# Second block: gate products in eight 384-column tiles, latents' products over two pairs of PSUM banks, first products of a turned tile reordered, bias rows turned one tile later

## The reference, cut to what matters

```python
c_act = jax.nn.silu(c)                                  # c: (1, 1024)
ada = c_act @ w_ada[l] + b_ada[l]                       # w_ada[l]: (1024, 6144)
sh1, sc1, gt1, sh2, sc2, gt2 = jnp.split(ada, 6, axis=-1)
```

```python
h = rmsnorm(x, ln_mix_g[l])
proj = h @ w_in[l]                                      # 1024 x 4128
ya = dilated_window_attention(qa, ka, va, bias_a)       # 8 heads of 64
yb = differential_attention(q1, q2, k1, k2, vb, lam, bias_b)   # 4 heads, two softmaxes each
qc = rmsnorm(cq, mla_q_norm_g[l]) @ w_uq[l]             # 768 x 768
kvc = rmsnorm(ckv, mla_kv_norm_g[l]) @ w_ukv[l]         # 256 x 1024
yc = mla_attention(...)                                 # 8 heads
gates = jax.nn.sigmoid(h @ w_gate[l] + b_gate[l])       # 1024 x 3072
merged = gates[0] * (ya @ w_br_a[l]) + gates[1] * (yb @ w_br_b[l]) + gates[2] * (yc @ w_br_c[l])
x = x + merged @ w_o[l]
```

## Time and profile before

| what | value |
|---|---|
| median of 3 runs | 1841.11 us (1839.01 to 1841.4) |
| time of the profiled execution | 1840.13 us |
| its span | 1838.3 us |
| PE / DVE / ACT / POOL busy | 96% / 69% / 48% / 3% |
| HBM read, mean rate | 343.69 MB, 188 GB/s |
| mean granted TensorE clock | 0.998 |

### The profile page before, as it was taken

The page is one execution under the profiler, slowest core; times in us unless marked ns, Lnnn a source line. Parts: engine busy times, 40 slices in busy tenths (PEclk is TensorE's granted clock), DMA queues, the critical chain, the costliest instruction groups (busy, mean ns, idle before and its releaser), DMA issues.

```text
span 1838.3 us, 26917 instructions
## 1 busy us (share of the span) xinstructions
PE 1761.9 (96%) x9090; PEld 1427.5 (78%) x9090; DVE 1272.3 (69%) x1949; ACT 889.8 (48%) x1506; POOL 55.7 (3%) x111
## 2 busy tenths in 40 slices
PE   7999999998999999999999999999999999999998
PEld 3775778986766789988987677788789877778886
DVE  5688897668788875566547887555555578865555
ACT  1456335443465344444655664444455556544443
POOL 0000010000000000002000000000000000000000
PEclk9999999999999999999999999999999999999999
DMA  8866568764765576645664334555556643345553
GB/s 306 260 222 207 178 223 291 257 218 147 236 220 193 182 233 210 209 158 155 190 217 156 119 98 149 187 180 183 179 166 181 219 137 126 112 150 186 183 181 128
DMA packets 212237, 346.12 MB, mean 188 GB/s; under 512 B 19915, under 2 KB 97273, under 8 KB 211881
## 3 DMA queue, kind: packets, MB, share of 16 engines
q1 hardware_dynamic: 208760, 338.89, 57.1%
q0 software_dynamic: 1632, 5.39, 1.0%
q10 hardware_dynamic: 1746, 0.54, 0.1%
HBM read 343.69 MB, written 1.07 MB: 188 GB/s over the span
## 4 chain that ended last, share of the span: by engine, by line
issue 80%; PE 12%; DVE 4%; DVEq 1%; POOLq 1%; POOL 1%; ACT 1%; DMA 0%; SPq 0%; ACTq 0%
PE acc L150 2%; PE acc L148 2%; PE acc L149 2%; PE prod L199 1%; PE prod L200 1%; PE prod L201 1%; DVE w_lo L134 1%; PE prod L148 1%; PE prod L150 1%; PE prod L149 1%; DVEq L908 1%; DVE proj L909 1%; DVE x_res L909 0%; DVE x_res L907 0%; ACT w_hi L128 0%
## 5 line engine op out<-in xcount | busy, mean ns | idle before, releaser
L134 DVE TENSOR_TENSOR w_lo<-w_raw,w_hi 128x1024 fp32r<-128x1024 f32 (+3 forms) x568 | 642.0, 1150 | 337.9 <-ACT w_hi L128 332.9
L128 ACT CAST w_hi<-w_raw 128x1024 fp32r<-128x1024 f32 (+3 forms) x568 | 556.3, 992 | 423.7 <-PE acc L150 171.5
L148 PE MATMUL prod<-w_hi,hT_hi 128*128 128x512 f32 (+1 forms) x880 | 331.1, 376 | 8.6 <-ACT proj_b L1912 2.2
L150 PE MATMUL prod<-w_hi,hT_lo 128*128 128x512 f32 (+1 forms) x880 | 323.1, 367 | 0.0
L149 PE MATMUL prod<-w_lo,hT_hi 128*128 128x512 f32 (+1 forms) x880 | 322.0, 366 | 0.0
L148 PEld LDWEIGHTS prod<-w_hi,hT_hi 128*128 128x128 f32 x880 | 165.7, 188 | 41.2 <-DVE w_lo L134 8.2
L150 PEld LDWEIGHTS prod<-w_hi,hT_lo 128*128 128x128 f32 x880 | 165.8, 188 | 24.0
L149 PEld LDWEIGHTS prod<-w_lo,hT_hi 128*128 128x128 f32 x880 | 166.3, 189 | 21.2
L148 PE MATMUL prod<-w_hi,uT_hi 128*128 128x512 f32 x368 | 152.1, 413 | 10.8 <-DVE w_lo L134 7.7
L150 PE MATMUL prod<-w_hi,uT_lo 128*128 128x512 f32 x368 | 145.8, 396 | 0.0
L149 PE MATMUL prod<-w_lo,uT_hi 128*128 128x512 f32 x368 | 145.7, 396 | 0.0
(11 more groups left out here) (332 smaller groups left out, 2681.5 us busy)
## 6 DMA issues: line engine op xcount, KB each, us to landing
w_raw<-in_w_in_dram SPq DMA_DIRECT2D x72, 512.0 KB, 3.8
ada_raw<-in_w_ada_dram SPq DMA_DIRECT2D x68, 512.0 KB, 7.0
w_raw<-in_w_in_dram SPq DMA_DIRECT2D x192, 172.0 KB, 2.4
w_raw<-in_w_up_dram SPq DMA_DIRECT2D x64, 512.0 KB, 4.3
w_raw<-in_w_down_dram SPq DMA_DIRECT2D x64, 512.0 KB, 4.7
w_raw<-in_w_gate_dram SPq DMA_DIRECT2D x96, 256.0 KB, 3.1
w_raw<-in_w_ffn_gate_dram SPq DMA_DIRECT2D x88, 256.0 KB, 3.5
w_raw<-in_w_ffn_up_dram SPq DMA_DIRECT2D x88, 256.0 KB, 4.3
```

The lines of the kernel that those rows point to most:

```text
L128: act.copy(self.hi[:, s, 0:cols], self.raw[:, s, 0:cols]).then_inc(self.hi_done, 1)
L134: dve.tensor_tensor(self.lo[:, s, 0:cols], self.raw[:, s, 0:cols], self.hi[:, s, 0:cols].bitcast(F32), ALU.subtract).then_inc(self.lo_done, 1)
L148: pe.matmul(out, a_hi, w_hi, start=first and c == 0, stop=False)
L150: mm = pe.matmul(out, a_lo, w_hi, start=False, stop=last and c == chunks - 1)
```

## The change

Six edits, all in the order or the width of work; what is computed is the same.

1. `w_gate` is cut into eight tiles of 384 columns (`GW`), one for each of the eight pairs and heads of A and B. Beside each stand four groups of 12 products. In B the next head's q and k are turned after the second group, and the probabilities after the third. PE's loop over the pairs of A is written out.
2. The tiles of `w_uq` go to `acc[0:2]` and `acc[2:4]`, those of `w_ukv` to `prod` and `acc[2:4]` (`up_banks`). The wait before them and the three identity products are gone. The turn of the first pair's probabilities, which writes to `acc[2:4]`, waits for the second `w_ukv` tile to be taken.
3. Layer 0: the fifth `w_in` tile runs before the eight bias rows are reversed, its weights are loaded before `flip`, the bias rows and the vectors, and the eight identity products are gone. The other four rows are reversed after the sixth tile; ACT's and DVE's copies move along.
4. `part_in_turn`, used at all eight turned tiles: within a group the two high-by-high products come first and wait only for the high parts, then two with the weight's low part, then two with the low part of the turned rows.
5. c is loaded with eight neighbouring values to a partition, and chunk k of `w_ada` is rows 8 p + k: neighbouring partitions read rows that lie eight rows apart. Each descriptor is as long as before.
6. `take_tile` is given its banks.

```diff
+    def part_in_turn(self, pe, pos, lhs, k0, width, tok, out, first, last, hi_taken, lo_taken):
+        if tok == 0:
+            pe.wait_ge(self.hi_done, pos.count(1 + self.groups))
+        if hi_taken:
+            hi_taken()
+        for c in range(KG):
+            pe.matmul(out, a_hi[c], w_hi[c], start=first and c == 0, stop=False)
+        if tok == 0:
+            pe.wait_ge(self.lo_done, pos.count(RING + 1 + self.groups))
+        for c in range(KG):
+            pe.matmul(out, a_hi[c], w_lo[c], start=False, stop=False)
+        if lo_taken:
+            lo_taken()
+        for c in range(KG):
+            mm = pe.matmul(out, a_lo[c], w_hi[c], start=False, stop=last and c == KG - 1)
...
+            def ada_chunks(l, k, chunks, cols):
+                return dr["w_ada"][slice(l, l + 1), :, cols].rearrange("a (p k) n -> p (a k) n", p=P)[:, k:k + chunks, :]
...
-            act.dma_start(c_col[:, :], dr["c"].rearrange("a (k p) -> p (a k)", p=P),
-                          allow_slow_non_contiguous=True).then_inc(first_in, 16)
+            act.dma_start(c_col[:, :], dr["c"].rearrange("a (p k) -> p (a k)", p=P)).then_inc(first_in, 16)
...
+GW, GATES = 3 * D // (PAIRS + BH), PAIRS + BH
+        up_banks = [acc[0:2], acc[2:4], prod, acc[2:4]]
...
                 for t in range(LAT_TILES):
                     in_tile(IN2_T - LAT_TILES + t, layer(l, 4 * t, G2))
+                in_tile(0, layer(l, 4 * LAT_TILES, G2))
                 if l == 0:
                     sp.wait_ge(first_left, 1)
                     sp.dma_start(flip, dr["flip"]).then_inc(consts_in, 16)
...
-                with sp.Fori(0, 6) as t:
+                with sp.Fori(0, GATES) as t:
                     for g in range(4):
-                        rows(Pos(G2_GATE + g, (l, G2), (t, 4)), ws["w_gate"], g * KG * P, bass.ds(t * NT, NT), NT)
+                        rows(Pos(G2_GATE + g, (l, G2), (t, 4)), ws["w_gate"], g * KG * P, bass.ds(t * GW, GW), GW)
...
# vector, branch B
-                    split(nxt + (-1), 2)
+                    split(nxt + (-1), 1, KG * GW)
+                    split(nxt, 2, KG * (GW if b < BH - 1 else NT))
                     if b > 0:
                         branch_b_lo(b - 1)
-                    if b % 2:
-                        add_gate_bias(gate_tile(l, 4 + b // 2), nxt + (-3), slice(2 * D + b // 2 * NT, 2 * D + (b // 2 + 1) * NT))
+                    split(nxt + 2, 1, KG * (GW if b < BH - 1 else NT))
+                    add_gate_bias(gate_tile(l, PAIRS + b), nxt + (-1), slice((PAIRS + b) * GW, (PAIRS + b + 1) * GW))
...
# tensor
-                    reverse_bias(range(4))
-                    T.awake(pe, layer(l, F2_LAT, F2), 8)
...
+                tile(layer(l, 4 * LAT_TILES, G2), layer(l, LAT_TILES, N2), uT, 0, 4, IN2_W)
+                if l == 0:
...
+                    reverse_bias(range(4))
+                tile(layer(l, 4 * LAT_TILES + 4, G2), layer(l, LAT_TILES + 1, N2), uT, 0, 4, IN2_W)
...
-                vacated(layer(l, N2_UQ, N2))(0)
-                for _ in range(3):
-                    pe.matmul(prod[0][:, 0:SEQ], ident, ident.unsqueeze(1).to_broadcast([P, 2, P]), start=True, stop=True)
...
-                with pe.Fori(0, PAIRS) as t:
+                for t in range(PAIRS):
...
-                    W.multiply(pe, this, uT, 4 * e, NT, KG, outs(NT), e == 0, False,
-                               vacant=vacated(gate_tile(l, 4 + b // 2)) if e == 0 else None)
+                    W.multiply(pe, this, uT, 0, GW, KG, outs(GW), True, False, vacant=vacated(gate_tile(l, PAIRS + b)))
+                    W.multiply(pe, this + 1, uT, 2, GW, KG, outs(GW), False, False)
                     if b < BH - 1:
                         qk_turns(n + 1, qk_turn(l, m + 1))
...
+                    W.multiply(pe, this + 2, uT, 4, GW, KG, outs(GW), False, False)
...
-                    W.multiply(pe, this + 1, uT, 4 * e + 2, NT, KG, outs(NT), False, e == 1, between=turn_p)
+                    W.multiply(pe, this + 3, uT, 6, GW, KG, outs(GW), False, True)
```

More of the change, by code:

```diff
@@ L165, in multiply, with turned_tile @@
                 between()
-    def turned_tile(self, pe, pos, lhs, width, outs, turn, taken, vacant, awake, before, after):
+    def turned_tile(self, pe, pos, lhs, width, outs, turn, taken, vacant, awake, before, after, halved):
         awake(0, before)
@@ L248, in awake, with halved @@
             pe.matmul(self.bank[b][:, 0:SEQ], self.ident, self.ident.unsqueeze(1).to_broadcast([P, 2, P]), start=True, stop=True)
+    def halved(self, eng, split):
+        eng.wait_ge(self.hi, split.count(1 + self.splits))
     def taken(self, eng, pos):
@@ L2016, in scalar @@
                 for j in range(2):
-                    split(layer(l, G2_GATE + 2 * j, G2), 2)
+                    split(layer(l, G2_GATE + 2 * j, G2), 2, KG * GW)
                     take_tile(layer(l, N2_UKV + j, N2), layer(l, G2_UKV + 2 * j + 1, G2),
-                              [kv_up[:, tok, j * NT:(j + 1) * NT] for tok in range(TOKS)], NT)
+                              [kv_up[:, tok, j * NT:(j + 1) * NT] for tok in range(TOKS)], NT, up_banks[2 + j])
                 with act.Fori(0, PAIRS) as t:
@@ L2041, in scalar @@
                     m = PAIRS + b
-                    n, nxt = pair(l, m), layer(l, G2_GATE + 20 + 2 * b, G2)
+                    n, nxt = pair(l, m), layer(l, G2_GATE + 20 + 4 * b, G2)
+                    cols = KG * (GW if b < BH - 1 else NT)
                     H.exps(act, n, 0)
                     H.exps(act, n, 1)
+                    split(nxt, 1, cols)
                     if b < BH - 1:
@@ L2268, in vector @@
                 split(layer(l, G2_UKV, G2), 4, NT)
[L2269 removed]
+                split(layer(l, G2_GATE, G2), 4, KG * GW)
                 rope_q = lambda: rope(dve, q_up.rearrange("p t (h e) -> p t h e", h=HEADS)[..., NOPE:QH],
```

159 lines of the change are left out of this document (85 added, 74 removed).

## The result

The changed kernel took 1824.96 us in the median of 4 runs (1822.69 to 1827.29), the kernel before 1840.06 beside it: the ratio is 0.992, 95% interval 0.9901 to 0.9939. Run once more, as a yardstick for the experiments, it took 1822.09 (ratio 0.9904, 0.9889 to 0.9919). The forecast was 1825, range 1814 to 1834. The profiled execution took 1823.75 us with a span of 1822.0, 16.3 less than before.

What follows compares the result with a forecast made beforehand. PE, busy 96% of the span, was taken as the bound. Start -0.5, turned tiles -2.5, bias rows -1.3, latents -6.0, gate tiles -7.4, handovers +1.6 sum to -16.1: 1824.0 profiled, 1825 as median, range 1814 to 1834.

Steps and rivals of the forecast that it cites:

- Gate tiles: Pairs of A and heads of B with 384-column gate tiles: -3.7 us a layer, -7.4 for two.
- rival 1: Heads of B become bound by DVE or ACT, 12.5 us instead of 11.5; half of its +11 gives 1831; chance 0.15.
- Heads: Four heads of B: 37.9 + 11.3 of added products - 3.4 of PE idle time = 45.8 us, +7.9.
- The last pair: Last pair of A: 13.1 us plus 0.8 more waiting for the rotation of q on DVE, 13.9.
- Latents: Start of `w_uq` -1.2 us and the `w_ukv` wait -1.8: -3.0 a layer, -6.0 for two.
- Bias rows: Layer 0, fifth tile before the reversal: a hole of 2.8 us replaces one of 4.1, -1.3.
- The hole: PE's gap ahead of the sixth `w_in` tile: load lands at 881.7, product starts at 884.5, hole 2.8 us.
- a bound of 0.7: Bias rows: 0.7 us more if the clock falls in the hole as in the earlier trace's rows 9.
- Turned tiles: Asking for low parts later hides waits: four places at 0.47 us and one at 0.6, -2.5.
- the other three: Three of the eight turned-tile places, counted as no gain because another engine paces them.
- Start: c's many packets leave the dense first loads that PE waits for: -0.5 us.
- The third rival: The 192 KB pitch of `w_ada` slows its first loads; at half the rate 1846 us; chance 0.04.

Runs made afterwards that it cites:

- the experiment with the banks: The changed kernel with `w_uq` and `w_ukv` in `prod` again, with the wait and three identity products: 1830.38 us, ratio 0.9941.
- the experiment with `b_gate`: The changed kernel with `b_gate` and the FFN's norm vector loaded behind `w_uq` instead of ahead of it: 1822.97 us, ratio 0.9902.
- hole filled: The changed kernel with seven identity products behind the first eight bias rows, ahead of the sixth tile: 1826.20 us, ratio 0.9911.

## Why the prediction was right

**Gate tiles.** The step is confirmed. The distance of 0.176 gave 11.5 for a middle pair and it takes 11.75; the wait for the probabilities is gone; DVE at 91% is not the bound, so rival 1 fell. Heads were forecast at 45.8 and are 44.34: by the forecast's own sum 37.90 + 11.3 - 44.34 = 4.9 us went, not 3.4. I took B's idle time as 3.4 from the busy sums of the earlier trace rows, in which the tails of products count as busy. Read by starts, the distances beyond the usual one of each kind of product shrink by 4.4 us in that stretch, and the 384-column products stand 0.173 apart there, which is the other 0.5 (192 x 0.003). The last pair was given 13.9 and takes 13.94, because the wait for the rotation grew from 1.3 to 2.4. What I did not see is that a wait of this length halves the clock behind it in some executions, 1.5 us: in the ten traces that have this wait it did so in ten of twenty such pairs, eight of layer 1 and two of layer 0.

**Latents.** The mechanism is right, and so is its size: the experiment with the banks has 1.2 us ahead of `w_uq` (forecast 1.2) and 1.9 at `w_ukv` (forecast 1.8) in layer 0, 1.5 and 1.8 in layer 1. The table's 4.4 is more because the start of `w_uq` is not as fixed as I took it from the earlier trace rows. It was late because ACT waited for weights behind 2 MB of broadcast vectors, which the experiment with `b_gate` shows, and that time moves from trace to trace: 0.9 and 1.9 us behind the last `w_in` product in the two layers of the first trace, 1.6 and 1.1 in the yardstick.

**Bias rows.** The hole came as forecast: load at 881.7 forecast, 880.7 measured; product at 884.5 and 883.80; hole 2.8 and 3.5. (The sum for the load has a slip: four groups of 12 x 0.157 are 7.5 us, not 6.8. The load came sooner all the same.) The step that failed is the clock. I charged nothing for it and gave its price only as a bound of 0.7, which was misread: the earlier trace rows hold half of that fall, and the whole cost 1.7. It fell behind this hole in every trace that has it and not where the hole was filled. From the first product behind the hole to the last of `w_in` it takes 56.98 us without a fall (one trace, hole filled), 58.2 to 58.5 in four traces with a short fall and 59.1 to 59.7 in five with a long one: 1.2 to 2.7 us. Against the kernel before, the edit's stretch thus grew by 0.6 instead of shrinking by 1.3. Against the same kernel with the old place it still gives something, by the traces, since the clock fell there too, 60 us later; how much is open. The rule of the Trainium skill that I had weighed ("TensorE: Matmul & The Clock Gate", Part 1: The HAM clock gate; an idle array falls to 1.2 GHz and activity releases it) agrees with this hole. I had set it aside on one wait of 1.65 us that left the clock whole.

**Turned tiles.** -2.5 was forecast for five places, 4.2 measured in seven. In the five places counted it is 2.8, so the mechanism and the size of one place hold, h of layer 0 (0.6) included. What failed is the sentence that the other three are paced by another engine: it is so for h of layer 1, and not for the first block's FFN tiles, which gave 0.7 each.

**Start.** The -0.5 agrees with the traces that can be compared (0.6 to 0.7), which are few. The +1.7 of the first trace is the chance of its clock.

**The third rival** fell too. "DMA: Bandwidth & Descriptors", section "Latency and other measured facts", of the Trainium skill lists lower rates for rows 512 KiB apart and more; it has no value for 192 KB. The landings above, 8.9 us in either layout, show no loss.

So the mechanisms were mostly right, but that the total agreed to the microsecond is luck. By the table latents and turned tiles gave 3.4 more than forecast and the pairs 1.0 more, the start and the bias rows 4.1 less, most of that from a clock at its lower level of 1.2 GHz, which I had charged at nothing. The same kernel run again came 3 us lower.

## What to carry to other kernels

Where one engine is the bound, price an edit by the distance between its instructions and by the gaps in starts, not by busy sums. When a step is moved in an in-order queue, its transfers move with it: look for the wide broadcasts and small vectors in front of the next weights, and for takes that stand behind late casts. And count a new wait of TensorE of 2 us or more at more than its length: in this kernel the half clock behind such waits cost another 1.2 to 2.7 us, in every trace for the longest of them and in about half for the others.

## What the runs showed of the hardware

- The wait at the sixth tile (PE idle for 2.9 to 4.4 us) was followed by half clock in all nine traces that had it, and by the PEclk column the fall cost 1.7 us in four of them and 3.4 in five. The wait of 2.4 us in the last pair of A was followed by it in ten cases of twenty, with no difference in the work. Filling the hole kept the clock whole there, and in that one trace it fell at the next long wait.
- A third such place is the second `w_in` tile of layer 1. With the new order of the turned tile PE waits 2.0 us ahead of it, for ACT, in all twelve traces, and the clock fell behind it in five. With the old order the wait is 1.7, and the clock stayed whole in both traces. The yardstick:

```profile
1339.56 0.63 PE L148 MATMUL prod<-w_hi,hT_hi 128*128 128x344 f32 x1 [2.05 <-ACT proj_b L1946]
```

- Near 180 and 580 us there are two gaps of 1.2 and 0.9 us close together, the same in the kernel before. One of the two places was hit in nine of the thirteen traces, and none in that of the kernel before. Why is open; with one trace of that kernel, chance isn't excluded.
- The records of the granted clock start late, at 4.5 to 23.1 us of the fourteen traces. Before the first of them PEclk shows 1.00, also where the same product takes twice as long.
